# Storing the high and the low part of each weight side by side instead of in two tiles

## The reference

```python
mod = silu(c) @ w_ada + b_ada                       # 6 x 1024 modulation values
h = rms_norm(x, norm1_w) * (1 + scale1) + shift1
proj = h @ w_in                                     # q, k, v, xBC, z, dt, gates
merged = g_attn * (attention(q, k, v) @ w_attn_out) + g_ssd * (ssd(xBC, z, dt) @ w_ssd_out)
x = x + gate1 * (merged @ w_o)
x = x + gate2 * (square(relu(h2 @ w_mlp1)) @ w_mlp2)            # 1024 -> 4096 -> 1024
# second block
u = rms_norm(x, norm1_w_2) @ w_in_2                 # six groups of 512 columns
h = x + concat(diff_attention, stick_breaking) @ w_out_2
out = h + (silu(u2 @ w_gate_2) * (u2 @ w_up_2)) @ w_down_2      # 1024 -> 2816 -> 1024
```

## Time and profile before

| what | value |
| --- | --- |
| median of 3 runs | 922.19 us |
| the three runs | 919.66, 922.19, 927.25 us |
| span of the profiled execution | 926.9 us (the profile gives no other time of it) |
| TensorE busy with matmuls | 903.5 us, 97% |
| TensorE busy with weight loads | 859.7 us, 93% |
| VectorE busy | 668.4 us, 72% |
| ScalarE busy | 512.5 us, 55% |
| granted TensorE clock, mean | 0.996 |

### The profile page before, as it was taken

The page is one execution under the profiler, slowest core; times in us unless marked ns, Lnnn a source line. Parts: engine busy times, 40 slices in busy tenths (PEclk is TensorE's granted clock), DMA queues, the critical chain, the costliest instruction groups (busy, mean ns, idle before and its releaser), DMA issues.

```text
span 926.9 us, 18052 instructions
## 1 busy us (share of the span) xinstructions
PE 903.5 (97%) x7424; PEld 859.7 (93%) x7424; DVE 668.4 (72%) x918; ACT 512.5 (55%) x696; POOL 79.8 (9%) x56
## 2 busy tenths in 40 slices
PE   5999999999999999999999999999998999999998
PEld 3899998788888899999999999988898999999998
DVE  6877998997699988778766545555875856666642
ACT  2566666667878773445655443346576754444430
POOL 0133000010465330000000000000000000000000
PEclk9999999999999999999999999999999999999999
DMA  9764554766322237684755555544332435555650
GB/s 376 302 242 151 204 192 147 263 219 236 124 65 87 92 138 250 223 301 146 264 182 182 186 188 193 192 152 169 116 126 86 142 137 187 185 190 193 217 192 18
DMA packets 25084, 168.00 MB, mean 181 GB/s; under 512 B 2868, under 2 KB 4532, under 8 KB 5048
## 3 DMA queue, kind: packets, MB, share of 16 engines
q1 hardware_dynamic: 23760, 164.90, 50.4%
q10 hardware_dynamic: 1256, 2.12, 0.6%
HBM read 165.95 MB, written 1.06 MB: 180 GB/s over the span
## 4 chain that ended last, share of the span: by engine, by line
PE 78%; DVE 8%; ACT 7%; issue 3%; DMA 3%; POOL 0%; SPq 0%; DVEq 0%; ACTq 0%; POOLq 0%
PE bank L1864 77%; DVE wlo L1107 2%; ACT whi L573 2%; DMA raw<-w_stream 2%; DVE acc L1152 1%; DMA adas<-w_stream 1%; ACT kw__113 L822 1%; PE bank L2132 1%; DVE eb L1432 1%; ACT ew L789 0%; DVE sslo L1468 0%; DVE wlo L1117 0%; DVE cvt L1341 0%; DVE p L1319 0%; ACT prob L724 0%
## 5 line engine op out<-in xcount | busy, mean ns | idle before, releaser
L1864 PE MATMUL bank<-hhi,whi 128*128 128x256 f32 (+1 forms) x1364 | 384.5, 284 | 0.8 <-DVE hlo L1210 0.6
L1864 PE MATMUL bank<-hlo,whi 128*128 128x256 f32 (+1 forms) x1352 | 377.5, 280 | 0.0
L1864 PE MATMUL bank<-hhi,wlo 128*128 128x256 f32 (+1 forms) x1352 | 375.7, 280 | 0.0
L1107 DVE TENSOR_TENSOR wlo<-raw,whi 128x2048 fp32r<-128x2048 f32 (+1 forms) x130 | 299.0, 2301 | 101.1 <-ACT whi L573 99.2
L573 ACT ACTIVATE whi<-raw 128x2048 fp32r<-128x2048 f32 (+1 forms) x132 | 250.6, 1898 | 101.3 <-PE bank L1864 74.2
L1864 PEld LDWEIGHTS bank<-hhi,whi 128*128 128x128 f32 (+1 forms) x1364 | 256.3, 188 | 11.5 <-issue 10.4
L1864 PEld LDWEIGHTS bank<-hlo,whi 128*128 128x128 f32 (+1 forms) x1352 | 257.2, 190 | 0.1
L1864 PEld LDWEIGHTS bank<-hhi,wlo 128*128 128x128 f32 (+1 forms) x1352 | 253.6, 188 | 0.0
L1864 PE MATMUL bank<-fhi,whi 128*128 128x256 f32 x432 | 121.4, 281 | 0.0
L1864 PE MATMUL bank<-flo,whi 128*128 128x256 f32 x432 | 121.4, 281 | 0.0
L1864 PE MATMUL bank<-fhi,wlo 128*128 128x256 f32 x432 | 121.4, 281 | 0.0
(11 more groups left out here) (296 smaller groups left out, 1311.2 us busy)
## 6 DMA issues: line engine op xcount, KB each, us to landing
raw<-w_stream SPq DMA_DIRECT2D x147, 1024.0 KB, 4.9
adas<-w_stream SPq DMA_DIRECT2D x8, 1024.0 KB, 8.6
xres<-x_t SPq DMA_DIRECT2D x1, 1024.0 KB, 10.1
out<-oute SPq DMA_DIRECT2D x8, 128.0 KB, 3.4
tabs<-tabs_in_dram ACTq DMA_DIRECT2D x1, 641.0 KB, 8.5
tabs<-tabs_in_dram ACTq DMA_DIRECT2D x1, 512.0 KB, 3.7
hankel<-bucket_rows ACTq DMA_DIRECT2D x1, 512.0 KB, 10.9
cols<-cols_in_dram ACTq DMA_DIRECT2D x1, 325.0 KB, 8.0
```

The source lines that it names most:

```text
L1107: nc.vector.tensor_tensor(out=wlo[:, c % RING, 0:n], in0=raw[:, r % RING, 0:n], in1=whi[:, c % RING, 0:n].bitcast(f32), op=ALU.subtract)\
L1864: return nc.tensor.matmul(out, lhsT, rhs, start=start, stop=stop)
```

## The change

`whi` and `wlo` become the two halves of one tile, `wsp`, in turn element by element: word 0 of a slot is the high part of element 0, word 1 its low part, word 2 the high part of element 1, and so on. The names `whi` and `wlo` stay as views of it with a step of two words (eight bytes). The tile is as large as the two were. `mod` is placed ahead of it instead of behind `csil`, so `wsp` begins 192 bytes after the place where `whi` began, `csil` moves up by 192 bytes, and `mscale` and everything behind it, the activations among them, keep their addresses.

```diff
     raw = place("raw", [P, RING, CW], f32)
-    whi = place("whi", [P, RING, CW], f32r)
-    wlo = place("wlo", [P, RING, CW], f32r)
+    mod = place("mod", [P, 48], f32)
+    wsp = place("wsp", [P, RING, CW, 2], f32r)
+    whi, wlo = wsp[:, :, :, 0], wsp[:, :, :, 1]
     csil = place("csil", [P, KD], f32)
-    mod = place("mod", [P, 48], f32)
     mscale = place("mscale", [P, 2 * KD], f32)
```

## The result

The changed kernel takes 948.04 us in the median (946.9 to 950.7, four runs) against 923.78 us for the kernel before in the same comparison: a ratio of 1.025, 95% interval 1.019 to 1.031. It is slower by 24 us where no change was forecast.

The account below looks back on a forecast made before the run. TensorE was taken as the bound, its weight load filling each step without slack. Terms of 0 on TensorE, VectorE and ScalarE left the profiled 926.9 us and the median of 922 us; range 905 to 1,000 us.

Parts of the forecast that it names:

- Moving `mod`, `csil` and the start of the ring by 192 bytes ... Nothing, 0 us: Placement of tiles: same instructions and sizes, `mod` read by short instructions only, so the shift costs 0 us.
- TensorE's loads, 6,324 of them, now step by eight bytes ... I take zero: Weight loads in L1864: stepped reading bounded between zero and 104 ns a load, taken as 0.
- the load alone sets it: TensorE's load and matmul pairs: the load, 113 ns from load to load, is already as long as the whole step.
- VectorE's zero: VectorE's 130 splits: stepped reading and writing add 0, bounded above by 1.66 us a split, 3.3 if both operands pay.
- ScalarE's zero: ScalarE's 132 rounding copies: stepped writes add 0, or at most 1.66 us on top of 1898 ns.
- 4 ns a load are 25 us: TensorE's 6,324 loads: even this small extra per load would decide the result.
- the second rival: TensorE's loads in L1864 pay up to 104 ns each, 658 us; from some 950 up to 1,580 us; 14%.
- The first: VectorE's splits, with or without ScalarE's copies, pay; TensorE doesn't; 940 to 1,000 us, thinly up to 1,100; 19%.
- The third: TensorE's pitch locks in one level: fast, near 906 us, 6%; slow, near 930 us and at most 935, 4%.
- the two levels: TensorE's pitch for the same work: 117.8 ns in the second feed-forward product, 113 ns in xbc.
- From below: TensorE's stepped load: the moving operand's 1024 bytes enter within 113 ns, so the load's extra cost may be zero.
- From above: TensorE's stepped load: priced like VectorE's 32-byte steps, 0.81 ns a word, it is 104 ns longer.

Follow-up runs that it names:

- D: Layout number: distance from the start of the weights (`whi`) to the start of the activations (`hhi`) within 256 bytes; 192 in the kernel before, 0 in the changed kernel.
- at 192: Distance of the kernel before, 923.78 us; also plain tiles with weights and activations both up by 64 bytes against it: 929.6 us, 1.004.
- at 200: Plain tiles, weights up by 24 and activations up by 32 bytes against the kernel before: 933.83 us, 1.013.
- 0 and 96: Plain tiles against the kernel before: 0 with activations up by 64 bytes, 945.24 us, or weights up by 192, 946.68 us; 96 with weights up by 96, 946.58 us.
- D = 224: Plain tiles, weights as before and activations up by 32 bytes against the kernel before: 936.95 us, 1.015.

## Why the prediction was wrong

**What failed.** Two steps of the part on the change, each enough by itself. "Moving `mod`, `csil` and the start of the ring by 192 bytes ... Nothing, 0 us" cost some 25 us when done alone. I priced the shift by who reads the small tiles that move, and left out that the ring moves against the activations. "TensorE's loads, 6,324 of them, now step by eight bytes ... I take zero" failed as well: done alone at the old place, the interleaving cost 28 us. The right term is about 3.4 ns a product on average: 2.2 ns where the pitch was 117.8 and 6.7 ns where it was 113.3. The two costs don't add, since both end at 120 ns; the changed kernel pays once. That the 948 us lie between the 905 and 1,000 us of the prediction is luck: that part of the range was there for slow splits that TensorE waits for, and neither happened.

**What held.** Nothing hides the pitch, so any change of the pair goes to the end 6,324 times: 3.4 ns were enough for 2.5%. That the load alone sets it was too simple: a load alone has 113 ns, yet m2 ran at 117.8 before, and plain pairs run at up to 120 by the distance. How long a stepped load takes with next to nothing streamed beside it wasn't run. VectorE's zero was right (2314 ns), so its rival, with up to 1.66 us more a split, is out. ScalarE's zero was 0.2 us a copy and hidden. Nothing new waits. "4 ns a load are 25 us" was nearly the result, but I had attached it to a price per word bounded by 104 ns, so that the small price of the second rival got no weight of its own.

**The rivals.** The first is out. The second had the sign that was seen, loads of `wsp` more than 118 ns apart in m2 with TensorE nearly always busy, and its stepped load does cost by itself; it says nothing of the shift, and its 104 ns were far too many for eight bytes. The third came nearest for the shift: a pitch that depends on how loads and matmuls fall against each other. Its two errors: it took the two levels seen as the only ones, so its slow side ended at 935 us, and it argued that "addresses aren't what chooses" because both levels occur with the same tiles. That observation was right and the conclusion wrong. The distance goes with the levels that a layout shows; which of them a stretch falls into is settled by something else.

**The bounds.** From below I argued that the moving side takes in 1024 bytes in 113 ns, so the stationary side might too. It did so in 120 ns. From above, the row of 32-byte steps named the right size for the case in which each word lies in other 16 bytes (0.89 against 0.81 ns a word), not for this one.

**The two rules.** By the 16-byte lines of the Trainium skill, "SBUF — State Buffer", section "Door 1: The DMA port swizzle", two hits in a line are enough for the full rate. VectorE at eight bytes agrees (2314 ns after 2301), and the leap of TensorE's loads at 16 bytes (113 ns more) fits. TensorE's loads at eight bytes don't agree: 120.0 ns where plain ones at the same place had 116.6 on average; nor do ScalarE's writes, at 0.10 ns a word more. By the rule of adjacent pairs of the Trainium skill, "Vector Engine (DVE) Microarchitecture Reference", section 5.2, a split would have become some 1.4 us longer, an estimate from its figures. It became 0.01 us longer, so the rule doesn't hold at a step of two words in this kernel.

## What to carry to other kernels

Where a stream of load and matmul pairs fills the time, treat the distance between the two operands' addresses within 256 bytes as a parameter of the kernel: it moved this one by up to 2.8%, and any small tile placed ahead of a ring can change it unseen. When a change has two parts, do each alone at the place of before. Here removing the step while the shift stayed showed no difference, and would have acquitted a part that costs as much as the whole. Keep a load's words next to each other: a step of 16 bytes about doubled the pitch, from 120 to 233 ns.

## What the runs showed of the hardware

- With the layout of two plain tiles the mean pitch of 128 columns loaded and 256 streamed ranged from 116.5 to 120.0 ns with D. Eight bytes made a difference: at 192 nearly all stretches ran at 113 or 118 ns, at 200 they lay between 116 and 119 with none at 113 (117.8 in the mean, ratio 1.013). That both operands are read from the same memory and meet there would explain it; this was not shown, nor why 0 and 96 are the worst.
- At D = 192 a stretch without other matmuls in between mostly keeps one level to its end: in the kernel before 454 steps from 94.3 us on at 113.4 ns, 1,378 from 446.5 us on at 117.8. The choice wasn't the same in the profiled runs of two kernels with this D and neighbouring words in the loads; whether it changes from one execution of a kernel to the next isn't shown, since each kernel has one trace. The single runs of the kernel before spread from 916 to 935 us. The granted clock doesn't order them: 917.3 us at 0.996 and 930.6 at 0.998 in one comparison. All products in the fast level or all in the slow one differ by 6,324 x 4.5 ns = 28 us, so the levels may be much of that spread, and the four runs at D = 224, where none is at 113 ns, lie within 0.8 us. What chooses stays open, and a layout with the fast level throughout, worth some 905 us by estimate, was not found.
- Stepping the written operand by eight bytes cost ScalarE 0.10 ns a word (1898 to 2103 ns, and 1897 with the shift alone), while VectorE, reading and writing in such steps at once, paid next to nothing (2301 to 2314 ns).
